# Changing the opening of an expert-row stream: the ring's first buffers, the place of the query-weight loads, and the order of work around rows 0 to 11

## What is computed

```
x = x + g1 * y_lat                                   # y_lat = merged @ w_out
h = modulate(x, norm_ffn_g, sh2, sc2)
q = (h @ w_query).reshape(128, 8 heads, 2, 128)
s = einsum('mhpd,hpnd->mhpn', q, sub_keys)           # two times 128 keys
top 16 of each half, 256 sums, top 16 of the sums  -> 16 experts idx, gate g (softmax)
act = gelu(einsum('mhkd,md->mhk', expert_u[idx], h))
out = einsum('mhk,mhkd->md', g * act, expert_v[idx])
x = x + g2 * out
```

## Time and profile before

| | |
|---|---|
| median of 3 runs | 1267.8 us |
| time of the profiled execution | 1268.92 us |
| its span, first to last instruction | 1267.0 us |
| busy: TensorE, VectorE, ScalarE, GpSimd | 90%, 68%, 25%, 26% |
| mean granted TensorE clock | 0.990 |
| gathers (software queue q0) | 269.63 MB |
| weights and inputs (hardware queue q1) | 118.59 MB |
| DMA over the span | 307 GB/s |

### The profile page before, as it was taken

The page is one execution under the profiler, slowest core; times in us unless marked ns, Lnnn a source line. Parts: engine busy times, 40 slices in busy tenths (PEclk is TensorE's granted clock), DMA queues, the critical chain, the costliest instruction groups (busy, mean ns, idle before and its releaser), DMA issues.

```text
span 1267.0 us, 14106 instructions
## 1 busy us (share of the span) xinstructions
PE 1140.1 (90%) x4824; PEld 696.8 (55%) x4824; DVE 865.2 (68%) x2320; ACT 311.8 (25%) x1005; POOL 331.8 (26%) x285
## 2 busy tenths in 40 slices
PE   9999999989999999999999899999777777777777
PEld 6866658767856678786656454554232323323322
DVE  2758735566445787863897777777778777777665
ACT  0125300244111232421232222232222222222222
POOL 0000000000011000000444544545644544454430
PEclk9999999999999999999999999999999999999999
DMA  8851256833145566454999999999999999999995
GB/s 337 312 202 67 100 199 253 309 112 133 67 199 196 208 216 227 191 194 173 373 377 423 423 424 423 423 423 424 424 423 424 423 423 424 423 423 423 423 424 215
DMA packets 54022, 389.10 MB, mean 307 GB/s; under 512 B 8088, under 2 KB 9624, under 8 KB 14784
## 3 DMA queue, kind: packets, MB, share of 16 engines
q0 software_dynamic: 37792, 269.63, 51.4%
q1 hardware_dynamic: 16160, 118.59, 24.6%
HBM read 387.12 MB, written 1.07 MB: 306 GB/s over the span
## 4 chain that ended last, share of the span: by engine, by line
PE 52%; DMA 34%; DVE 10%; ACT 2%; issue 1%; POOL 0%; SPq 0%; DVEq 0%; ACTq 0%
PE bank L566 15%; PE bank L560 13%; DMA wring<-peer_uv_in,arena 11%; DMA arena<-peer_uv_in,arena 9%; PE bank L1153 9%; DMA const<-peer_uv_in,arena 8%; DMA hT<-peer_uv_in,arena 5%; PE bank L1048 2%; PE bank L595 2%; PE bank L968 2%; DVE arena L1644 1%; PE bank L641 1%; DVE arena L1652 1%; PE bank L627 1%; PE bank L791 1%
## 5 line engine op out<-in xcount | busy, mean ns | idle before, releaser
L1153 PE MATMUL bank<-arena 128*128 128x512 f32 x424 | 202.6, 609 | 40.9 <-ACT arena L1609 40.8
L1153 PE MATMUL bank<-wring,arena 128*128 128x512 f32 x376 | 179.1, 610 | 38.8 <-ACT arena L1609 38.8
L566 PE MATMUL bank<-hT,wring 128*128 128x256 f32 (+1 forms) x896 | 172.5, 351 | 1.0 <-ACT arena L1393 1.0
L2442 POOL TENSOR_TENSOR small<-small,const 128x1 f32<-128x1 f32 (+3 forms) x18 | 16.7, 927 | 566.8 <-DVEq L1656 260.1
L2371 DVE CUSTOM_DVE_ANT_0 arena<-arena 128x1024 f32<-128x1024 f32 x106 | 129.3, 1223 | 50.8 <-DMA arena<-peer_uv_in,arena 50.6
L566 PEld LDWEIGHTS bank<-hT,wring 128*128 128x128 f32 x896 | 150.2, 190 | 24.3 <-issue 8.4
L1153 PEld LDWEIGHTS bank<-arena 128*128 128x128 f32 x424 | 78.2, 194 | 150.4 <-issue 80.8
L2481 POOL DMA_INDIRECT arena<-peer_uv_in,arena x104 | 124.8, 1200 | 132.9 <-PE bank L1153 110.8
L2371 DVE CUSTOM_DVE_ANT_0 wring<-wring,arena 128x1024 f32<-128x1024 f32 x94 | 114.7, 1221 | 44.0 <-DMA wring<-peer_uv_in,arena 43.8
L2481 POOL DMA_INDIRECT wring<-peer_uv_in,arena x94 | 113.9, 1211 | 110.1 <-PE bank L1153 98.8
L1153 PEld LDWEIGHTS bank<-wring,arena 128*128 128x128 f32 x376 | 68.3, 191 | 134.7 <-issue 69.9
(11 more groups left out here) (250 smaller groups left out, 1526.7 us busy)
## 6 DMA issues: line engine op xcount, KB each, us to landing
wring<-w_in SPq DMA_DIRECT2D x22, 2048.0 KB, 8.2
wring<-ada_in SPq DMA_DIRECT2D x12, 2048.0 KB, 9.2
wring<-wo_in SPq DMA_DIRECT2D x5, 2048.0 KB, 7.9
wring<-br_in SPq DMA_DIRECT2D x2, 2048.0 KB, 9.3
arena<-pq_in SPq DMA_DIRECT2D x2, 2048.0 KB, 9.8
wring<-w1b_in SPq DMA_DIRECT2D x2, 1120.0 KB, 8.8
const<-const_in SPq DMA_DIRECT2D x1, 2188.5 KB, 17.8
arena<-cmp_in SPq DMA_DIRECT2D x2, 1024.0 KB, 10.9
```

The costliest lines, as they stand in the source:

```text
L566: ins = pe.matmul(bank[:, at:at + n_tok], w[:, k, col:col + P], rhs[:, k, :], start=(k == 0), stop=(k == KC - 1))
L1153: ins = pe.matmul(sums_of[half][:, :], diag[:, at % NDIAG, :], v_row[slot_of[at]][:, half * 512:(half + 1) * 512], start=(n == 0), stop=(n ...
```

## The change

Seven things change together.

- **The ring** opens with six buffers at row 0: ONCE, 0, BRANCH_SLOT, GATES_SLOT and the two of ("wo2", 0, 0). The two of ("wo2", 0, 1) come at row 7, the two under query chunk 0 at row 37, 78 as before, number 5 at 95, two at 112, three at 122. LAST_EARLY no longer belongs to the ring.
- **Query chunk 3** is loaded in two halves into buffers 5 and 17, one right behind the first half of chunk 2, one after the second mT transposes (`full(sp, ("mT", 1))`). Chunk 2 and chunk 3 change places in the second tile's pieces.
- **`mrgT`** moves from the arena's end to two pieces under `h2` (`mrg_of`), and VectorE's `branch_a(2)` comes behind `latent(0)`.
- **`out_rows(1, 1)`** on TensorE comes behind row 1, as piece "out"; its VectorE share behind row 5 (before: row 1), and ScalarE's `x1_squares(1)`, which waits for that, behind the diagonals of rows 4 and 5.
- **VectorE** computes before row 0 only what head 0's gate weights need (`first_weights`). Indices and decoding of head 0's second eight, and `out_rows(0, 1)`, come behind row 1 (`rest_of_first`), the gate weights between rows 0 and 1.
- **Head 2 alone, and head 3**: scores of one head each ("hs", h) at rows 7 and 17 in place of ("ps", 0, 1) at row 9. "head1" moves from row 1 to 3, "pT" from 11 to 15, the q pieces by up to six rows.
- **Head 1's choice** lies at row 9 (parts 0 to 7) and row 11 (parts 8 to 15).

```
 
-            p = place[chunk][0]
+            p = place.get(chunk, (None,))[0]
             if chunk == ("pq", 0, 2):
                 return [7 + 2 * p, QUERY_SLOT]
+            if chunk == ("pq", 0, 3):
+                return [5, SCORE_SLOT]
             return {IN_CONST: [6, 16], IN_ARENA: [1, 2]}.get(p, [7 + 2 * p, 8 + 2 * p])
 
-        LAST_EARLY, QUERY_SLOT, GATES_SLOT, ONCE = 17, 4, 3, 18
+        SCORE_SLOT, QUERY_SLOT, GATES_SLOT, ONCE = 17, 4, 3, 18
         BRANCH_SLOT = 8 + 2 * place[("br", 0, 1)][0]
-        freed_by = {n: ("wo2", 1, 1) for n in [5] + slots_in(("wo2", 0, 1))}
+        freed_by = {n: ("wo2", 1, 1) for n in slots_in(("wo2", 0, 1))}
         freed_by.update({n: ("wo2", 0, 1) for n in slots_in(("wo2", 0, 0))})
-        freed_by.update({n: ("pq", c, 3, 1) for c in (1, 2, 3) for n in slots_in(("pq", 0, c))})
+        freed_by.update({n: ("pq", c, 3, 1) for c in range(4) for n in slots_in(("pq", 0, c))})
         freed_by.update({n: ("ps", 1, 3) for n in (13, 14, 15)})
         freed_by.update({n: ("bm", 1, 1) for n in (0, BRANCH_SLOT)})
-        new_slots = {0: [LAST_EARLY, ONCE, 0, BRANCH_SLOT, GATES_SLOT] + slots_in(("wo2", 0, 0)) + [5] + slots_in(("wo2", 0, 1)),
-                     78: slots_in(("pq", 0, 1)), 95: slots_in(("pq", 0, 2)), 112: slots_in(("pq", 0, 3)), 122: [13, 14, 15]}
+        new_slots = {0: [ONCE, 0, BRANCH_SLOT, GATES_SLOT] + slots_in(("wo2", 0, 0)), 7: slots_in(("wo2", 0, 1)),
+                     37: slots_in(("pq", 0, 0)), 78: slots_in(("pq", 0, 1)), 95: [5], 112: slots_in(("pq", 0, 2)), 122: [13, 14, 15]}
         slot_of, use_no, last_user, fresh = [], [], {}, []
         for n in range(ROWS):
             fresh += new_slots.get(n, [])
-            if n == 70:
-                last_score = last_user.pop(LAST_EARLY)
             if fresh:
                 r = fresh.pop(0)
             else:
...
         pieces = {}
-        plan = [(1, ("head1",))] + [(row, ("q", 1, n + 1, 0)) for n, row in enumerate((3, 5, 7))] + [(9, ("ps", 0, 1)), (11, ("pT", 1))]
-        plan += [(row, ("q", 2, n, 0)) for n, row in enumerate((13, 17, 21, 25))] + [(29, ("ps", 0, 2))]
-        plan += [(row, ("q", 0, n, 1)) for n, row in enumerate((15, 19, 23, 27))]
-        plan += [(row, ("q", 3, n, 0)) for n, row in enumerate((35, 39, 43, 47))] + [(49, ("ps", 0, 3))]
-        plan += [(row, ("q", 1, n, 1)) for n, row in enumerate((51, 55, 59, 63))]
-        plan += [(row, ("q", 2, n, 1)) for n, row in enumerate((67, 71, 75, 79))]
+        plan = [(1, ("out",)), (3, ("head1",)), (5, ("q", 1, 1, 0)), (7, ("hs", 2))]
+        plan += [(11, ("q", 1, 2, 0)), (13, ("q", 1, 3, 0)), (15, ("pT", 1)), (17, ("hs", 3))]
+        plan += [(row, ("q", 2, n, 0)) for n, row in enumerate((19, 23, 27, 31))] + [(33, ("ps", 0, 2))]
+        plan += [(row, ("q", 0, n, 1)) for n, row in enumerate((17, 21, 25, 29))]
+        plan += [(row, ("q", 3, n, 0)) for n, row in enumerate((37, 41, 45, 49))] + [(51, ("ps", 0, 3))]
+        plan += [(row, ("q", 1, n, 1)) for n, row in enumerate((53, 57, 61, 65))]
+        plan += [(row, ("q", 3, n, 1)) for n, row in enumerate((67, 71, 75, 79))]
         plan += [(83, ("h2", 1, 0)), (85, ("ps", 1, 0)), (87, ("ps", 1, 1))]
-        plan += [(row, ("q", 3, n, 1)) for n, row in enumerate((89, 91, 93, 95))]
+        plan += [(row, ("q", 2, n, 1)) for n, row in enumerate((89, 91, 93, 95))]
         plan += [(99, ("ps", 1, 2)), (103, ("ps", 1, 3))]
         for row, piece in plan:
...
         for n in range(16):
-            choice_at.setdefault(5 + n * 5 // 16, []).append((1, n))
+            choice_at.setdefault(9 if n < 8 else 11, []).append((1, n))
         for h in range(2, TT * EH):
...
                         pe.wait_ge(sem("mrg"), 2 * t + k // 4 + 1)
-                    ins = pe.matmul(bank[:, :], mrgT[:, k, t * P:(t + 1) * P], w[:, k, :], start=(k == 0), stop=(k == KC - 1))
+                    ins = pe.matmul(bank[:, :], mrg_of[t][:, k, :], w[:, k, :], start=(k == 0), stop=(k == KC - 1))
                 finish(ins, ("wo2", half, t))
...
                     if at + 1 == ROWS or group_of[at + 1] != group_of[at]:
                         for piece in filler(group_of[at]):
-                            if piece[0] == "head1":
+                            if piece[0] == "out":
+                                out_rows(1, 1)
+                            elif piece[0] == "head1":
                                 head_queries(1)
                                 queries(1, 0, 0)
+                                taken(pe, ("pq0", 1))
                                 head_scores(1)
+                            elif piece[0] == "hs":
+                                for b in range(2):
+                                    taken(pe, ("pq", 1, 2 * (piece[1] % 2) + b, 0))
+                                head_scores(piece[1])
                             elif piece[0] == "q":
                                 queries(*piece[1:])
...
                     sp.dma_start(pair[high], a["pq"][2][:, 2 * D:4 * D]).then_inc(sem("in_pq2_1"), 16)
+                    for part, n in enumerate(slots_in(("pq", 0, 3))):
+                        if part:
+                            full(sp, ("mT", 1))
+                        sp.dma_start(pair[n], a["pq"][3][:, part * 2 * D:(part + 1) * 2 * D]).then_inc(sem(f"in_pq3_{part}"), 16)
                     full(sp, ("bm", 0, 1))
                     sp.dma_start(pair[low], a["pq"][2][:, 0:2 * D]).then_inc(sem("in_pq2_0"), 16)
                     continue
-                elif chunk == ("pq", 0, 3):
-                    full(sp, chunk_last[("pq", 0, 0)])
                 elif chunk == ("cmp", 1, 0):
                     full(sp, chunk_last[("wo", 0, 1)])
...
                     act.activation(diag[:, (at + r) % NDIAG, :], ident, ACT.Copy, scale=wcur[:, w:w + 1]).then_inc(sem("diag_ready"), 1)
-                if g == 0:
+                if at == 4:
                     x1_squares(1)
                 for piece in filler(g - 1) if g else []:
+                    if piece[0] == "out":
+                        continue
                     if piece[0] == "head1":
...
                     else:
-                        if piece == ("ps", 1, 0):
-                            act.wait_ge(sem("row_used"), last_score + 1)
                         key_scores(*piece[1:])
                 for row in range(at, at + size):
...
                              ALU.mult, ALU.add), "mlstm_s")
-                    if i in (4, 5, 6):
+                    if i in (4, 5):
                         branch_a(i - 4)
                     if i == 5:
...
                 else:
-                    dve.wait_ge(sem("scores"), 1 if head == 1 else head // 2 + 1)
+                    dve.wait_ge(sem("scores"), head if head < 4 else head // 2 + 2)
                 if part == 0:
...
                         result(0)
-                    if at == 4:
+                    if at == 0:
+                        choice_weights(0)
+                    if at == 8:
                         rms_begin(sumsq[:, 1:2], 6)
-                    if at == 6:
+                    if at == 12:
                         rms_end(h2, 1)
                     due += choice_at.get(at, [])
...
+                        rest_of_first()
+                    if at == 5:
                         out_rows(1, 1)
                 if head + 1 < TT * EH:
...
 
+            def first_weights():
+
+                step(dve.max(tops[:, 8:TOPK], work_a))
+                step(dve.max(tops[:, TOPK + 8:2 * TOPK], work_b))
+                settle()
+                step(tt(cand.rearrange("p (a b) -> p a b", a=TOPK), every(tops[:, 0:TOPK], TOPK, 2),
+                        every(tops[:, TOPK:2 * TOPK], TOPK), ALU.add))
+                ts(esum[:, 0:1], best[:, 0:1], -1.0, ALU.mult).then_inc(sem("top_neg"), 1)
+                settle()
+                step(dve.match_replace(work, best[:, 0:8], cand, -3e38))
+                settle()
+                step(dve.max(best[:, 8:TOPK], work))
+                settle()
+                dve.wait_ge(sem("top_neg"), 1)
+                dve.sem_inc(sem("top_sub"), 1)
+
+            def rest_of_first():
+
+                step(dve.max_index(topi[:, 8:TOPK], tops[:, 8:TOPK], work_a))
+                step(dve.max_index(topi[:, TOPK + 8:2 * TOPK], tops[:, TOPK + 8:2 * TOPK], work_b))
+                step(dve.max_index(bpos[:, 8:TOPK], best[:, 8:TOPK], work))
+                settle()
+                step(dve.tensor_copy(topf, topi))
+                decode(TOPK // 2, "idx_ready")
+                out_rows(0, 1)
+
             first_eight()
             merge(1, 1)
-            for part in (3, 4, 5):
-                choose(0, part)
-            settle()
-            step(dve.match_replace(work, best[:, 0:8], cand, -3e38))
```

29 lines of the change are left out of this document (12 added, 17 removed).

## The result

The changed kernel took 1275.2 us (median of 6 runs, 1274.09 to 1277.28) beside 1267.94 for the kernel before on the same chip: a ratio of 1.0058, 95% interval 1.0045 to 1.0071. Measured again on a second chip it took 1273.06 (8 runs, 1270.36 to 1275.51), ratio 1.0031 (1.0020 to 1.0042). Slower both times. The forecast was 1270.0. The profiled execution took 1274.58 us, its span is 1272.7 (before 1267.0).

A forecast was written before the change was run, and what follows sets the result against it. TensorE was taken to set the pace in the first 38 rows, DMA behind them. Early load and thinner ring, followed to row 36, gave +2.1 us on 1268.92; less 1.1 for the median, 1269.9, rounded to 1270, range 1263.5 to 1274.5.

The forecast's parts named there:

- The stream and its account: Behind the first 38 rows the DMA stream stays full near 424 GB/s, so time lost or won ahead decides the end.
- chunk 3's 4.95 us: Loading query chunk 3 early, near 569 and 576 us, takes it out of the full stream at 695: -4.95 us.
- The idle of TensorE: Ahead of row 28: gaps of 2.2, 0.6 and 3.5 us, plus 1.5 added, 7.8 us against about 1.2 before.
- The step that failed: From 650.5 us to row 28's release: 48.2 us of TensorE work plus 1.5, so release at 700.2.
- the added 1.5: Extra TensorE idle put on rows 12, 13 and rows 18, 19, 1.5 us, called the weakest figure.
- The landing of row 35: Row 35's gather, issued at 700.6, lands 7.3 us later at 707.9, with bounds of 5.6 and 8.2.
- the 2.5 of the working: At row 36's landing, 710.4 against 707.9 before, the changed kernel stands 2.5 us behind.
- the rounding to 2.1: The sum of 2.5 us at row 36 rounded down to +2.1 us, the added idle being the weakest figure.
- rival 2: Ahead of row 35, the seven-buffer round from gather to release closes on VectorE: 1272.6 us, up to 1275.3; chance 0.25.
- Rival 1: Between rows 8 and 28 the ring doesn't bind and TensorE loses nothing: faster, 1264.3 us; chance 0.20.
- Rival 3: Two rows fewer ahead and two rows' worth of load gone, 4.95 us each, cancel: 1267.8 us; chance 0.20.
- The gather's price: For one gather the skill page fits 2.0 us plus bytes / 436 GB/s, 4.4 us; the sum would be -0.4 us.

The follow-up runs named there:

- e8: Kernel before with the change's thin ring in the old order of work, query chunk 3 loaded as late as before: 1276.32 us, ratio 1.0047.
- e1: Kernel before with the change's ring, early load of query chunk 3 and moved merged rows, but the old order of work: 1272.1 us, ratio 1.0027.
- e16: Changed kernel with the products of rows 7 and 9 made twice, to fill TensorE's gaps: 1274.68 us, ratio 1.0048.
- e17: Changed kernel with row 7's products made twice and row 9's three times, to fill TensorE's gaps: 1274.87 us, ratio 1.0044.
- e18: Changed kernel with nothing edited, timed on the chip of e16 and e17: 1273.06 us, ratio 1.0031 to the kernel before.
- e4: Changed kernel with one buffer fewer from row 7 to row 36, six in the ring: 1280.07 us, ratio 1.0092.
- e5: e1 with the second tile's four q pieces of chunk 0 moved behind rows 69 to 81: 1271.09 us, ratio 1.0010.
- e11: e6 with the second tile's four q pieces of chunk 0 moved behind rows 69 to 81: 1271.29 us, ratio 1.0010.
- e6: Changed kernel with head 1's choice spread over rows 7, 9 and 11 (6, 5, 5 parts) instead of 9 and 11: 1270.35 us, ratio 1.0006.
- e7: Changed kernel with output half 1 of the second tile back in front of row 0: 1273.62 us, ratio 1.0030.
- e10: Kernel before with only the change's new order, and head 1's choice over rows 7, 9 and 11: 1276.3 us, ratio 1.0057.

## Why the prediction was wrong

**The stream and its account: right.** The loss lies ahead of row 37, the rate is 423 GB/s behind it, and chunk 3's 4.95 us lie within what e8 against e1 leaves open, 2.5 to 5.7.

**The idle of TensorE: right in place, short by one pair in size.** Row 16's gather was forecast near 649.9 and came at 650.28. Rows 10 and 11 were forecast to start at 650.5 and started at 650.57, behind 3.04 us of idle (forecast 3.5), with VectorE's choice named. Head 1's choice was followed correctly through both lumps. On the way row 1's landing took 5.6 us, not the 6.7 taken over from the earlier trace rows, so TensorE was early and stood idle for 2.14 us ahead of row 8 instead of 0.6: the diagonals were there when forecast, at 643.8.

**The step that failed** is the one behind it: "From 650.5 to the release of row 28 TensorE has 19 rows x 1.72 + 8 q pieces x 1.78 + 0.87 + 0.46 = 48.2 us, and I add 1.5 us". It took the full clock for granted. The first pair ran at half of it, 6.77 us and not 3.44: +3.3, and the added 1.5 didn't come. Row 28 was released at 702.1, not at 700.2. So much is in the profile. That the kernel gets faster where the clock stays up is not shown: the medians of e16 and e17 didn't fall. That TensorE works at one of two levels, 1.2 and 2.4 GHz, and falls to the lower one behind idle time, is in the Trainium skill, "TensorE: Matmul & The Clock Gate", section "Part 1: The HAM clock gate (the "warmup" mystery)"; the traces agree, 6.77 / 3.44 is 1.97. The forecast had put two gaps close together and never asked what the clock would do behind them.

**The landing of row 35: a term undersized.** Forecast 7.3 between bounds of 5.6 and 8.2; measured 8.2, the upper bound. The path was wrong here too: it let the stream fill behind row 35, and the landings show it full from row 31's on, at 700.6. Row 35's 8.2 us were spent behind the rows ahead of it, so it doesn't hang on row 28's release alone, and the split that follows is that of the forecast's sum. The two together give 1.8 for the issue (702.41 against 700.6) + 0.9 = 2.7 us, which with the 2.5 of the working are the 5.2 us seen at row 37. In the rounding to 2.1, 0.4 more was lost; half a microsecond more came behind row 37. The median stood 0.6 above the profiled execution and not 1.1 below, as the one of before had.

**The range** ended at 1274.5, below rival 2's own upper value of 1275.3, and it had no term for the clock. By e18 the kernel's median on another chip lay inside it.

**Rival 1** (1264.3) fell: seven buffers do bind, by 8.1 us of span or 6.0 by the ratio for the ring alone (e8). The rule of the Trainium skill quoted with it, to double-buffer ("Trainium Kernel Development and Optimization", section "Best Practices"), would have seven, or six, be plenty; e4 shows six to be 5.1 us of span slower than seven. **Rival 2**'s upper value, 1275.3, is the measured time, but by luck. Its sign came: VectorE waits for gathers at rows 25 and 27 already. But TensorE has no gap from 654 to 699, and row 28 is released by TensorE's work, so the waits didn't reach the release. Its mechanism sets the pace in e4, and fits what is left in e5 and e11. **Rival 3**, the cancelling, is near what e6 shows once the lump is gone: the whole change within 0.1% of the kernel before. Ring and load alone leave 0.27% (e1). The gather's price by the Trainium skill, "DMA: Bandwidth & Descriptors", section "Anatomy of one DMA — SWDGE (gpsimd) path", an estimate of 4.4 us, is met by no landing that VectorE waited for here: 5.5 us at the least (row 6 of e7, row 7 of e4).

## What to carry to other kernels

Where three engines take turns on small pairs of work, look for the longest lump on the one in the middle: sixteen short parts of VectorE's work in two pairs instead of three cost 5.2 us of span here (3.2 to 6.6 us by the ratios), and one line took them back. When a change opens idle time ahead of TensorE, price the work behind the gap at both clocks, and add that to the range. And when two parts of a change pull on the same buffers and indices, price them together: the same order cost nothing on top of the ring of seven and the early load (e6 beside e1), and 0.57% with nine buffers and the late load (e10).
